# Narrow gate products turned round, Fox attention scaled ahead of its turn, and the first expert's rows picked on the chip

## What is computed

```
# block 1, layer 1: "Fox" attention, 16 heads of 64, causal, with a forget gate (16 logits per position)
q, k, v, f = split(rmsnorm(x) @ w_in)             # q, k, v: 1024 columns each, f: 16
q, k = rmsnorm of each head's 64 columns
F = cumsum(log_sigmoid(f + f_bias))               # per head
p = softmax(q @ k.T / 8 + F_i - F_j, causal)
x = x + (p @ v) @ w_o
# block 2: a mixer whose mLSTM branch has 8 gate logits per position
proj = rmsnorm(x) @ w_in                          # qk 2048, v 1024, gates i,f 8, and more columns
# block 2: mixture of experts, 32 experts, 2 chosen per position, rows sorted by expert
g_idx = argmax(xt @ w_rg + b_rg); e = top_k of the 8 logits of that group, 2
y = sum over the 2 chosen e of gate * (silu(x @ w1[e]) * (x @ w3[e])) @ w2[e]
```

## Time and profile before

| | us |
|---|---|
| median of 3 runs | 2711.86 (2709.64 to 2712.19) |
| the profiled execution | 2712.2 |
| its span | 2710.5 |
| PE busy | 2595.9 (96%) |
| DVE busy | 1496.3 (55%) |
| ACT busy | 1235.3 (46%) |
| chain that ended last, PE's share | 60% |

### The profile page before, as it was taken

One profiled execution on the slowest core, in us unless ns is written; L12 is line 12 of the kernel. 1 busy time (PEld: TensorE's weight loads), 2 busy tenths in 40 slices (PEclk: granted clock), 3 DMA queues, 4 the chain that ended last, 5 costly groups with the idle time before them and its releaser, 6 DMA issues.

```text
span 2710.5 us, 30491 instructions
## 1 busy us (share of the span) xinstructions
PE 2595.9 (96%) x12148; PEld 2121.8 (78%) x12148; DVE 1496.3 (55%) x2018; ACT 1235.3 (46%) x1583; POOL 110.7 (4%) x162
## 2 busy tenths in 40 slices
PE   7999999999999999999999999989995999999995
PEld 6767888888887777888888778878874888888884
DVE  5577543344333554434466444354355888888885
ACT  3387322223335732222323333333343777777773
POOL 0111000000330000000000000000001000000001
PEclk9989999999898999999999999999997999999997
DMA  4301233433430033242322132221307999999993
GB/s 141 124 1 32 78 111 131 136 97 118 140 100 33 1 117 109 94 155 94 124 94 80 45 110 90 104 94 65 124 1 280 376 406 407 409 407 405 407 405 134
DMA packets 157046, 432.26 MB, mean 159 GB/s; under 512 B 11083, under 2 KB 80870, under 8 KB 144486
## 3 DMA queue, kind: packets, MB, share of 16 engines
q1 hardware_dynamic: 148870, 400.87, 40.1%
q10 hardware_dynamic: 4736, 16.81, 1.5%
q0 software_dynamic: 3296, 12.58, 1.2%
HBM read 383.06 MB, written 47.19 MB: 159 GB/s over the span
## 4 chain that ended last, share of the span: by engine, by line
PE 60%; DVE 2%; ACT 1%; DMA 1%; issue 1%; POOL 0%; ACTq 0%; POOLq 0%; DVEq 0%
PE ps L312 12%; PE ps L313 12%; PE ps L314 12%; PE ps L2469 7%; PE ps L2467 7%; PE ps L2468 7%; PE ps L929 1%; PE ps L2449 1%; PE ps L1914 1%; PE ps L2494 1%; PE ps L2190 0%; DVE area L337 0%; ACT area L331 0%; DMA area<-expert_rows,rowu 0%; PE ps L918 0%
## 5 line engine op out<-in xcount | busy, mean ns | idle before, releaser
L337 DVE TENSOR_TENSOR area<-area,area 128x2048 fp32r<-128x2048 f32 (+4 forms) x161 | 340.4, 2115 | 594.5 <-ACT area L331 594.5
L314 PE MATMUL ps<-area,area 128*128 128x512 f32 (+1 forms) x1696 | 658.1, 388 | 0.0
L331 ACT ACTIVATE area<-area 128x2048 fp32r<-128x2048 f32 (+4 forms) x161 | 284.4, 1767 | 595.0 <-PE ps L314 586.6
L313 PE MATMUL ps<-area,area 128*128 128x512 f32 (+5 forms) x1432 | 552.2, 386 | 0.0
L2440 DVE TENSOR_TENSOR area<-area,area 128x2048 fp32r<-128x2048 f32 x192 | 433.3, 2284 | 74.9 <-ACT area L2435 65.5
L312 PE MATMUL ps<-actT_parts,area 128*128 128x512 f32 x968 | 383.8, 396 | 5.1 <-DVE area L813 1.9
L313 PE MATMUL ps<-actT_parts,area 128*128 128x512 f32 x968 | 382.8, 395 | 0.0
L2435 ACT ACTIVATE area<-area 128x2048 fp32r<-128x2048 f32 x192 | 360.7, 1912 | 36.5 <-PE ps L2469 17.7
L314 PEld LDWEIGHTS ps<-area,area 128*128 128x128 f32 x1696 | 320.3, 189 | 68.9
L313 PEld LDWEIGHTS ps<-area,area 128*128 128x128 f32 x1432 | 278.6, 195 | 52.6
L312 PE MATMUL ps<-area,area 128*128 128x512 f32 (+2 forms) x728 | 278.8, 383 | 11.4 <-DVE area L705 11.4
(11 more groups left out here) (327 smaller groups left out, 3174.6 us busy)
## 6 DMA issues: line engine op xcount, KB each, us to landing
area<-in_w SPq DMA_DIRECT2D x96, 2048.0 KB, 9.6
area<-in_w_in SPq DMA_DIRECT2D x16, 2048.0 KB, 7.8
area<-in_l_w_gate SPq DMA_DIRECT2D x22, 1024.0 KB, 5.4
area<-in_l_w_up SPq DMA_DIRECT2D x22, 1024.0 KB, 8.0
expert_inputs<-maskz SPq DMA_DIRECT2D x39, 512.0 KB, 8.6
area<-in_l_w_in SPq DMA_DIRECT2D x9, 2048.0 KB, 8.3
area<-expert_inputs SPq DMA_DIRECT2D x32, 512.0 KB, 9.8
expert_rows<-area ACTq DMA_DIRECT2D x32, 512.0 KB, 9.6
```

The source lines that it names most:

```text
L313: pe.matmul(dst(r), a.l, b.h, start=False, stop=False)
L314: m = pe.matmul(dst(r), a.h, b.l, start=False, stop=end)
L331: eng.activation(w.h, raw, ACT.Copy).then_inc(w_hi, 1)
L337: dve.tensor_tensor(w.l, raw, w.high_f, ALU.subtract).then_inc(w_lo, 1)
```

## The change

1. **Gate columns likewise.** The two narrow products become `Thin` jobs, a form of `Cols`: the 16 (8) weight columns are stationary and 512 positions move, 24 matmuls. ACT copies the 16x512 result out (`take_act`), PE turns it in four pieces (`turn_pe`, placed between the two pieces of product 2), and DVE reads the turned values where it read the product.
2. **Fox attention.** A new class `Columns`: DVE scales the exponentials in `Pb` by the reciprocal of their sum before PE turns them, the values are stationary (a pair of heads, 128 columns) and the turned probabilities move (128 columns), so a head's output appears by features, four units in one bank. ACT and DVE split it once per head straight into the parts `oT` that the out product reads. The `out_stage` with its turns goes for this layer, and so does the barrier ahead of it (`product_stage`). Q and K lie in another order in memory, and the first piece of `w_o` is split inside the loop.
3. **First expert.** The small tables and `xn` move to ring slots 3 and 4. The logits are turned right after the second group of `rows_pe`. DVE makes from expert 0's ranks four 0/1 matrices `chosen`, and PE makes expert 0's columns from `xn` with 32 matmuls (`first_rows_pe`), without device memory. Only 3 of the 5 slots are loaded ahead; expert 0's three matrices are the first three in the order. `m_is` counts to 2.

```diff
+        class Thin(Cols):
...
+            def operands(self, r, w, i, k):
+                return w[:, i, :], self.rhs[:, k, :]
...
+            def take_act(self, act, dst):
+                self.ready(act, 0)
+                act.activation(dst, self.src(0), ACT.Copy).then_inc(t_ev, 1)
+
+            def turn_pe(self, pe, rows):
+                pe.wait_ge(t_ev, self.c0 + 1)
+                self.gr.wait_free(pe, self.g0 + 1)
+                for t in range(NT):
+                    m = pe.transpose(self.turned(t), rows[:, t * P:t * P + P], ident[0:self.n, 0:self.n])
+                m.then_inc(t_tr, 1)
...
-                    job.pe(pe)
+                    job.pe(pe, None, (lambda pe: fj.turn_pe(pe, forget)) if job is qk_jobs[2][0] else None)
...
                     if c == 7:
                         msp.before(act, 2)
+                        ij.take_act(act, ifT)
                         msp.after(act, 2)
...
+        class Columns(Attention):
...
+            def pe(self, pe):
+                for v in range(self.units + 4):
+                    self.pe_preps(pe, v)
+                    self.pe_scores(pe, v)
+                    self.pe_turn(pe, v - 3)
+                    self.pe_values(pe, v - 4)
...
+                    for j in range(i + 1):
+                        m = pe.matmul(ps[:, self.vb[h % 2], i * P:i * P + P], self.pair_values(h, j),
+                                      self.PT[:, u % 2, j * P:j * P + P], start=(j == 0), stop=(j == i))
...
+                    h, i = divmod(v - 8, NT)
+                    if v >= 8 and i == 0:
+                        act.wait_ge(s_o, self.o0 + NT * h + NT)
+                        act.activation(self.oT.h[self.half(h), h // 2, :], self.gathered(h), ACT.Copy).then_inc(s_oh, 1)
...
+                    if 0 <= v - 1 < self.units:
+                        u = v - 1
+                        p = self.Pb[:, u % 4, 0:self.length(u)]
+                        dve.wait_ge(s_ex, self.ex0 + u + 1)
+                        ch(dve.reciprocal(col(rinv, u), col(rs, u)))
+                        dve.tensor_scalar(p, p, col(rinv, u), None, ALU.mult).then_inc(s_nm, 1)
...
+                        dve.tensor_tensor(d.l, self.gathered(h), d.high_f, ALU.subtract).then_inc(s_ol, 1)
...
+            def first_rows_pe(pe):
+                pe.wait_ge(m_xn, NT)
+                pe.wait_ge(m_sel, NT)
+                for half in range(2):
+                    for j in range(4):
+                        for t in range(NT):
+                            m = pe.matmul(ps[:, 2 + half, j * P:j * P + P],
+                                          xn[:, t, :].rearrange("p (s k) -> p k s", k=KD)[:, 4 * half + j, :],
+                                          chosen[:, t, :], start=(t == 0), stop=(t == NT - 1))
+                    m.then_inc(m_gt, 1)
...
             def ex_pe(pe, ch):
                 router_pe(pe)
-                turn_rows(pe, 0)
-                turn_rows(pe, 1)
+                first_rows_pe(pe)
                 for j in range(2):
                     for half in range(2):
                         up(pe, 0, j, half)
-                for n in range(NE):
+                turn(pe, 0)
+                down(pe, 0, 0)
+                turn_rows(pe, 1)
+                down(pe, 0, 1)
+                for half in range(2):
+                    up(pe, 1, 0, half)
+                turn_rows(pe, 2)
+                for half in range(2):
+                    up(pe, 1, 1, half)
+                for n in range(1, NE):
...
             def ex_act(act, ch):
...
                 cols_high(act, 0)
+                split_high(act, 4)
+                silu(act, 0)
+                split_high(act, 5)
+                split_high(act, 6)
+                turned_high(act, 0)
```

More of the change, by code:

```diff
@@ L2239, in bass_two_blocks_kernel @@
             hits = early_work(2912, NOVER, NE)
[L2240 removed]
+            xn = area(4 * SLOT, 0, NT, D)
+            chosen = early_work(3136, NT, P)
+            first_rank = early_work(3648, NT)
             rowu = sb("rowu", [P, 2 * NT], U32)
@@ L2480, in up @@
                         pe.wait_ge(m_hb, n)
+                if n == 0 and j == 0 and half:
+                    pe.wait_ge(m_gxl, 2)
                 pe.wait_ge(x_lo, p + 1)
```

250 lines of the change are left out of this document (189 added, 61 removed).

## The result

The changed kernel takes 2690.28 us (median of three; 2688.84 to 2690.79) against 2711.18 of the kernel before: a ratio of 0.9922, 95% interval 0.9902 to 0.9941. It is faster, by 20.9 us or 0.8%; 35.3 were forecast, and 2690.28 lies just outside the range that ends at 2690. A fourth execution of it took 4731 us at a mean granted clock of 0.80, was disturbed, and is left out. The profiled execution took 2689.8, with a span of 2688.1.

The account below looks back on a forecast made before the run. PE, busy 96% of the span, was taken as the bound. Fox gate -12.8, mixer -1.3, Fox attention -12.9 and first expert -8.3 sum to -35.3 against the profiled 2712.2: 2677 us, range 2665 to 2690.

Parts of the forecast that it names:

- Fox gate product: Fox layer's gate columns: 24 matmuls at 0.23 take 5.5 us in place of 17.07; sum -12.8 us.
- slow tail: Nine wide matmuls behind the Fox gate product take 3.80 us, not 2.07, at the lower clock; 1.7 us would go.
- Mixer: Mixer's gate columns: PE finishes early but waits 10 us for DVE's split ahead of product 2; sum -1.3 us.
- The end of Fox attention: After the last values: 7.3 us of barrier, turns and split go; 0.7 comes back for the deeper pipeline.
- The loop: Fox attention's heads: the 0.5 us wait in each goes, -6.8 us in all, with 0.5 back for the splits.
- Rival (c): Fox attention loop: DVE or ACT sets the pace; no gain, 2683, or 0.4 us per head worse, 2690; chance 0.14.
- The logits, the ranks, `m_done`: Start of experts: logits' turn 3.4 us earlier, ranks at 2063.9, the chain to `m_done` ends at 2070.8.
- The columns: Expert 0's columns: begin at 2065.2, 32 products take 8.8 us with a low clock at first, until 2074.
- The scatter: POOL starts at 2070.0; two queues share some 430 GB/s evenly with the weights, so it lasts till 2087.5.
- The rows of expert 1: They queue behind 4 MB of weights for 9.3 us and land at 2098; PE waits 5.3 us.
- rival (e): Experts: the weight stream never catches up, ending at 2635 to 2671, at worst 7 us past PE's 2664; chance 0.04.
- (d): Wide matmuls with 16 stationary columns lose the clock, +4, or experts' first weights come later, +6: 2681 to 2687; chance 0.10.

Follow-up runs that it names:

- plain columns: Changed kernel with expert 0's columns taken from 128 neighbouring features of `xn`, not every eighth, and two first weight matrices loaded in matching row order: 2699.86 us.
- rows first: Changed kernel with SyncE asking for expert 1's rows and matrix 4 ahead of matrices 5 and 6: 2684.94 us.
- rows first, early matrix 5: Changed kernel with expert 1's rows asked for ahead of matrix 6, and matrix 5 before the scatter begins: 2687.03 us.
- plain columns, rows first, early matrix 5: Changed kernel with columns from neighbouring features, expert 1's rows asked for earlier, and matrix 5 asked for before the scatter: 2683.19 us.
- the run with three edits: Changed kernel with ACT's copy later in Fox attention, the mixer's split ahead of the convolution, and expert 1's rows ahead of matrices 5 and 6: 2671.9 us.
- four edits: Changed kernel with later ACT copy, mixer split ahead of convolution, expert 1's rows earlier with matrix 5 before the scatter, and neighbouring-feature columns: 2670.99 us.

## Why the prediction was wrong, by its own steps

- **Fox gate product: right.** -12.8 forecast, -12.55 in the traces, 10.9 in the run that undid it. Full pace with 16 standing columns, the 0.1 us wait for DVE's split and the end of the slow tail were all there.
- **Mixer: right.** -1.3 forecast, -1.6 measured, 1.3 in the undo; the hole of 10 us and its releaser were as named, and an order that takes it away was worth 11.
- **The end of Fox attention: right.** The out product follows the values at once.
- **The loop: wrong, 8 us.** The step that failed is "Both fit in 6.35, ACT with the smaller margin". It compared busy time with the period: 5.10 + 0.6 against 6.35. ACT did have the room (5.54 of 6.90), but its new copy stood ahead of the one instruction for which PE waits, in a ring that closes in every head: scores, DVE's maximum, ACT's exponentials, the copy of the queries, PE's second preparation. Rival (c) named this outcome with a chance of 0.14, and its 0.4 us per head was too much: it was 0.12. With the copy one place later the stage took 113.0 us, and 126.08 less the forecast 12.9 is 113.2, so the rest of that sum was right in total. DVE's part was taken too small (1.0 more per head forecast, 1.7 measured in the run with the later copy, 5.3 against 3.6), which cost nothing.
- **The logits, the ranks, `m_done`: right**, each within 0.3 us, and POOL's start within 0.8.
- **The columns: wrong, 6.5 us.** The step that failed is "32 products: 7.1 us at 0.22", from a row whose standing operand is contiguous. Here it is read in steps of eight values, and a record costs 0.24 in place of 0.114 at the full clock; the low clock, for which 1.7 us had been added, was not the reason. With neighbouring features the same columns took 9.5 us, near the forecast 8.8.
- **The scatter: its time right within 1.0 us, by luck.** It landed at 2088.5 in the forecast's times, 2087.5 were forecast. The forecast let three matrices start with 2.7 MB of the scatter left and gave each queue half. (By its own numbers that is 12.6 us from 2076, 2088.6.) In the trace the matrices came 6.5 us later, with 0.70 MB left, which by halves is some 3 us of work; it took 8.0. The step that failed is the even share: it is even in packets, and in the run with plain columns the scatter got 1.02 of 5.12 MB. What held up the last packets of the scatter in the changed kernel, 21 of them in the 6 us from 2065 on, stays open. The two queues from 2062.9 to 2070.9:

```profile
q1 hardware_dynamic: 147, 2.23, 72.0%
q0 software_dynamic: 204, 0.70, 26.2%
```

- **The rows of expert 1: right in kind.** Queueing behind three matrices and the shared scatter were there. The rows landed 3.4 us later than forecast, with the matrices asked for 6.5 us later. Of the stage's miss of 4.8 us the run with plain columns shows that the columns themselves carry nothing while this order stands: the time of expert 1 is set by when the rows land. About 1 us is the wait for DVE at expert 1's turn, a term that the forecast put at nothing.
- **The weight stream, rival (e): did not occur.** No wait for weights is left in the experts; a period stays 18.07 us. Nor did the first half of (d): the granted clock is 1.00 over the Fox gate product.
- Of the 12.9 us between the forecast and the two spans, 9.6 lie in attention and 4.8 in the experts; the stretches that the change does not touch gave 1.5 back.

The Trainium skill, DMA: Bandwidth & Descriptors, on queues, rings and completion order, has each DMA engine take its queues in turn, a packet at a time. The run with plain columns agrees, 282 packets against 282 while both queues had work; the forecast's step from there to half of the rate does not follow, since the packets differ in size. How long the scatter takes, from POOL's first issue to SP's next one behind the landing, goes with what runs beside it and from when:

| run | matrices asked for | after POOL's first issue | scatter |
|---|---|---|---|
| kernel before | none | | 13.8 |
| rows first | one | 11.6 | 14.7 |
| rows first, early matrix 5 | one | 11.3 | 14.7 |
| changed kernel | two, a third 5.7 later | 11.3 | 19.3 |
| plain columns, rows first, early matrix 5 | one | 5.9 | 21.7 |
| plain columns | two, a third 5.7 later | 5.8 | 29.4 |

Where matrix 5 is early it was asked for 5.8 us ahead of POOL's first issue; by the second and third rows that alone costs the scatter nothing. Five more runs have the changed kernel's order: 19.2 to 19.4 us in three, and at most 17.4 and 17.6 in two, where SP itself came free only then.

## What to carry to other kernels

When a change gives an engine work, don't compare sums of busy time: find the instruction of that engine for which the critical engine waits, and see whether the new one stands ahead of it in the queue. Here one copy of 0.6 us cost 8 to 10 us of a stage by where it stood, and nothing that the traces show one place later. Count what a wait costs from start to start: here it was more than the idle time that the profile lists. Price a matmul from a row with the same layout of the standing operand, not only the same size. Before you let two DMA queues share, look at the size of their packets. And where an engine waits for a transfer, an earlier arrival of that engine is worth nothing until the transfer has been moved.

## What the runs showed of the hardware

- **A strided standing operand.** Loading 128x128 float32 values eight apart took 336 ns at a granted clock of 1.00 where contiguous ones took 192, and such products ran at 0.24 us a record in place of 0.114. At 0.50 the two took 338 and 333 ns: the strided load gained nothing from the full clock.
- **Two DMA queues share by packets, not by bytes.** With both busy, 282 packets of each moved in 12 us, 4.10 MB of weights against 1.02 MB of the scatter.
- **Few standing columns keep the pace.** 24 matmuls of 512 moving columns with 16 standing ones began 0.23 us apart at a granted clock of 1.00, as with 128; 96 with 16 moving ones were 0.11 apart for 3.5 or 5.4 us and 0.21 from then on, at 0.50.
- **The clock can come back late, and why is open.** In the first layer, which no run here edits, the granted clock returned to the upper level at some 160 us in some executions and after 200 in others, with the same work to do in each. Windows of the changed kernel, and of the run with three edits (clock is the third number from the right):

```profile
160.00:180.00 20.00, 19.69 (x129) 15.04 (x128) 18.11 (x55) 18.64 (x51) 3.15 (x12) 1.00 0.00 1
180.00:200.00 20.00, 19.74 (x127) 14.78 (x126) 17.22 (x56) 19.47 (x52) 3.34 (x13) 1.00 0.01 2
```

```profile
160.00:180.00 20.00, 20.00 (x68) 14.66 (x68) 10.22 (x30) 10.58 (x29) 1.61 (x6) 0.50 0.00 1
180.00:200.00 20.00, 20.00 (x71) 15.09 (x71) 10.22 (x32) 11.83 (x30) 1.61 (x6) 0.50 0.00 1
```

In the second PE gets through 68 and 71 matmuls in 20 us, in the first through 129 and 127. Counted where attention begins, it cost 20.6 us there, 7.7 in the run with plain columns, 6.6 in that with four edits, 13.2 where the old start of the experts was put back and 20.5 where the old attention was. The other runs with the changed gate products lie within 2.2 us of the changed kernel. What decides it stays open: no run was made for it, and it is not bound to one edit. A gain of 10 us in the whole time of this kernel can't be read from one execution, but can from the stage in its trace.
